# x handed over turned, the reciprocal root applied behind the projections, and a third of the weight rests moved to GpSimd

## The chip, the cores and the metric

The kernel runs on one core of a Trainium2 chip. The metric is the device time of one execution in microseconds (us). The kernel before takes 575.78 us, the median of three runs (575.1 to 575.89).

Five engines work side by side and meet at semaphores: TensorE (PE in the rows; PEld is its loading of weights), VectorE (DVE), ScalarE (ACT), GpSimd (POOL) and SyncE (SP), which here only starts transfers. Each takes its instructions in the order in which the program gives them.

## The reference, cut to what matters

One layer (512 tokens, width 1024): RMSNorm, one input projection, three groups of heads, one output projection, then a SwiGLU block. All data is float32.

```python
def hybrid_layer(x, ...):
    hn = rms_norm(x, g_pre_mix)      # x * rsqrt(mean(x*x) + 1e-6) * g
    proj = hn @ w_in
    mq, mk, mv, fq, fk, fv, f_logit, cvb, cvc, cvh = jnp.split(proj, SPLIT_IDX, axis=-1)
    moba = moba_attention(heads(mq, 6), heads(mk, 6), heads(mv, 6), rel_bias)
    log_f = jax.nn.log_sigmoid(f_logit + b_f)
    fox = forgetting_attention(heads(fq, 6), heads(fk, 6), heads(fv, 6), log_f)
    conv = cvb * causal_depthwise_conv3(cvc * cvh, conv_w)
    mixed = jnp.concatenate([merge(moba), merge(fox), conv], axis=-1) @ w_out
    x = x + rms_norm(mixed, g_post_mix)
    h2 = rms_norm(x, g_pre_ffn)
    ff = (silu(h2 @ w_gate) * (h2 @ w_up)) @ w_down
    return x + rms_norm(ff, g_post_ffn)
```

The root in the first norm is one number per token; g is one number per feature. So `hn @ w_in` is also `r * ((x * g) @ w_in)` with r per token, which is what the change uses.

## The kernel before, in words

Float32 products are made out of two rounded parts. Every operand is split into `hi` (rounded, made by ScalarE, or by GpSimd for the value weights) and `lo` (the rest, made by VectorE), and a product is three products on TensorE: hi*hi, hi*lo, lo*hi (`product`, L1663 to L1668). The splits are called `split(u)`: u counts units of weights, 0 to 2 are chunks of the value weights, 3 to 23 are 1024x128 slices of `w_in`, then come the slices of `w_out` and those of the SwiGLU weights. Units travel through four buffers `raw`, loaded by SyncE when the unit four places earlier has its `lo`.

The opening (up to the first logits) handles one tile of 128 tokens after another: ScalarE squares and takes the root (L752, L754), VectorE multiplies by the reciprocal root and g (`normalise`, L1126), TensorE turns the tile (`turn`, L1702), ScalarE and VectorE make `hn_hi` and `hn_lo` (L770, L1134) out of PSUM. TensorE then makes the values of the tile (`v_mm`, L1720, 128x390 outputs), and in between the four small products of the relative bias (L1688, L1690). g reaches all partitions through a product with a row of ones (L1681). Last come the q and k groups of the first pair of heads.

Attention works on six pairs of heads, three of the moba kind and three of the fox kind (forgetting attention), in 8 steps a pair; a step g is one head and one tile of 128 queries. At each step TensorE makes the logits (L1803, L1805), then three eighths of a projection group of the next pair as filler, then the product with the values where a head is complete (`pv`, L1827, in steps 2 and 6 of a pair) and the transposes of the probabilities of step g - 2 (L1815). VectorE adds the bias (L1297), makes `pT_lo` (L1231), scales the probabilities (L1331), and evacuates groups that are complete; ScalarE makes exp (L859), `pT_hi` (L806) and the splits. A pair's q group is complete in its step 2 and the k group in step 5: ScalarE writes the `hi` halves (L790, two instructions of 64 partitions), VectorE the `lo` halves (L1191, two). TensorE's first logits of the next pair wait for the k group and for two transfers that swap the halves of q (GpSimd's queue, L638 and L640). GpSimd also masks the bias of the fox pairs (L666, one block each) and starts the transfers of the bias. In the last pair the filler is the convolution's groups (`conv_tail`).

The order on each engine is written out by hand in the step loops; there is no scheduler. Behind attention come the output projection, the norms and the SwiGLU block, none of which the change touches beyond the names of the waits.

## Time and profile before

| what | value |
|---|---|
| time, median of 3 runs | 575.78 us |
| the profiled execution | 576.57 us |
| its span | 574.8 us |
| granted clock, mean | 0.998 |
| TensorE busy | 567.5 us, 99% |
| VectorE busy | 471.5 us, 82% |
| ScalarE busy | 319.7 us, 56% |
| GpSimd busy | 110.4 us, 19% |
| first logits of attention | 42.61 us |

The span runs from the first to the last instruction; the time of the execution has 1.8 us around it. A busy TensorE is not one at its peak, because matmuls are pipelined: of two products in a row the second starts long before the first ends. Their pitch, start to start, is the cost of one. In a timeline row the two first numbers are the start and the length in us; at its end stands the idle time of the engine before it and what ended it.

### The profile page before, as it was taken

The numbers are of one execution on the slowest core, as the hardware profiler recorded it, in microseconds if no ns is written. First come the engines' busy times: TensorE is split into PE (matmuls) and PEld (weight loads), VectorE is DVE, ScalarE is ACT, GpSimd is POOL, SyncE is SP. The second block draws the span as 40 slices with busy tenths as digits, with TensorE's granted clock in tenths as the row PEclk, the third lists the DMA queues.
The fourth block names the chain that finished last, engine by engine and source line by source line (L and its number), as shares of the span: only waits on it lengthen the run. The fifth ranks groups of instructions, "written<-read, shape, count | busy, mean of one in ns | idle before, by whom it ended". The sixth has DMA issues, their size and how long they took to land.

```text
span 574.8 us, 9664 instructions
## 1 busy us (share of the span) xinstructions
PE 567.5 (99%) x3372; PEld 502.8 (87%) x3372; DVE 471.5 (82%) x791; ACT 319.7 (56%) x539; POOL 110.4 (19%) x129
## 2 busy tenths in 40 slices
PE   8999999999999999999999999999999999999996
PEld 6988888888888888899999999999999988888884
DVE  5647888888797954799888988988898788888787
ACT  5625765766555645575545546454554565547762
POOL 3020001103220000000324242332324002233100
PEclk9999999999999999999999999999999999999999
DMA  8274334346312471302323223242322359999743
GB/s 331 85 214 136 91 105 132 95 141 185 110 48 100 147 299 68 111 38 75 144 76 131 88 75 144 73 145 74 144 75 81 138 188 268 269 211 199 167 146 146
DMA packets 23144, 78.92 MB, mean 137 GB/s; under 512 B 2972, under 2 KB 2972, under 8 KB 23114
## 3 DMA queue, kind: packets, MB, share of 16 engines
q1 hardware_dynamic: 16716, 57.44, 28.2%
q0 software_dynamic: 6304, 21.00, 16.1%
q8 instruction: 17, 0.28, 0.2%
q10 hardware_dynamic: 94, 0.09, 0.0%
q14 instruction: 13, 0.11, 0.0%
HBM read 71.16 MB, written 4.22 MB: 131 GB/s over the span
## 4 chain that ended last, share of the span: by engine, by line
PE 99%; DVE 0%; POOL 0%; issue 0%; DVEq 0%; ACT 0%; POOLq 0%
PE bank L1666 11%; PE bank L1668 11%; PE bank L1667 11%; PE bank L1951 8%; PE bank L1950 8%; PE bank L1949 8%; PE bank L1957 7%; PE bank L2019 6%; PE bank L2017 6%; PE bank L2015 6%; PE bank L1960 3%; PE bank L1720 3%; PE bank L1827 3%; PE bank L1815 2%; PE bank L1805 1%; PE bank L1803 1%
## 5 line engine op out<-in xcount | busy, mean ns | idle before, releaser
L1950 PE MATMUL bank<-tok_lo,form_hi 128*128 128x256 f32 x320 | 90.6, 283 | 0.0
L1951 PE MATMUL bank<-tok_hi,form_lo 128*128 128x256 f32 x320 | 90.6, 283 | 0.0
L1949 PE MATMUL bank<-tok_hi,form_hi 128*128 128x256 f32 x320 | 90.5, 283 | 0.0
L1666 PE MATMUL bank<-hn,w_hi 128*128 128x512 f32 (+1 forms) x200 | 76.6, 383 | 0.0
L1668 PE MATMUL bank<-hn,w_lo 128*128 128x512 f32 (+1 forms) x200 | 75.0, 375 | 0.0
L1667 PE MATMUL bank<-hn,w_hi 128*128 128x512 f32 (+1 forms) x200 | 74.6, 373 | 0.0
L1949 PEld LDWEIGHTS bank<-tok_hi,form_hi 128*128 128x128 f32 x320 | 60.9, 190 | 1.9
L1951 PEld LDWEIGHTS bank<-tok_hi,form_lo 128*128 128x128 f32 x320 | 61.1, 191 | 0.0
L1950 PEld LDWEIGHTS bank<-tok_lo,form_hi 128*128 128x128 f32 x320 | 61.0, 191 | 0.0
L2015 PE MATMUL bank<-dw_hi,da_hi 128*128 128x512 f32 x154 | 59.9, 389 | 0.0
L2019 PE MATMUL bank<-dw_hi,da_lo 128*128 128x512 f32 x154 | 59.9, 389 | 0.0
L2017 PE MATMUL bank<-dw_lo,da_hi 128*128 128x512 f32 x154 | 59.9, 389 | 0.0
L1957 PE MATMUL bank<-hn,form_hi 128*128 128x512 f32 x160 | 58.1, 397 | 0.0
L712 POOL TENSOR_TENSOR sum_f<-raw 128x512 f32<-128x512 f32 x18 | 27.8, 1544 | 144.9 <-DVE form_lo L1457 144.9
L1457 DVE TENSOR_TENSOR form_lo<-sum_f,form_hi 128x1024 fp32r<-128x1024 f32 x40 | 48.6, 1216 | 0.0
L1457 DVE TENSOR_TENSOR form_lo<-raw,form_hi 128x1024 fp32r<-128x1024 f32 (+1 forms) x40 | 47.0, 1175 | 0.6
L859 ACT ACTIVATE probs<-logits,neg_max 128x128 f32<-128x128 f32 (+3 forms) x48 | 27.1, 564 | 36.4 <-DVE neg_max L1297 36.4
L971 ACT CAST form_hi<-sum_f 128x1024 fp32r<-128x1024 f32 x40 | 42.0, 1053 | 6.2 <-DVE sum_f L1395 5.9
L1960 PE MATMUL bank<-hn,form_lo 128*128 128x256 f32 x160 | 44.9, 281 | 0.0
L1668 PEld LDWEIGHTS bank<-hn,w_lo 128*128 128x128 f32 x200 | 37.7, 188 | 7.2
L1666 PEld LDWEIGHTS bank<-hn,w_hi 128*128 128x128 f32 x200 | 37.7, 189 | 6.1 <-issue 0.9
L1667 PEld LDWEIGHTS bank<-hn,w_hi 128*128 128x128 f32 x200 | 37.8, 189 | 5.1
(206 smaller groups left out, 1397.0 us busy)
## 6 DMA issues: line engine op xcount, KB each, us to landing
raw<-in_w_gate_units SPq DMA_DIRECT2D x22, 512.0 KB, 3.6
raw<-in_w_up_units SPq DMA_DIRECT2D x22, 512.0 KB, 4.5
raw<-in_w_in_units SPq DMA_DIRECT2D x21, 512.0 KB, 3.3
down_x<-in_w_down POOLq DMA_DIRECT2D x15, 512.0 KB, 9.7
down_y<-in_w_down SPq DMA_DIRECT2D x10, 512.0 KB, 9.2
raw<-in_w_out SPq DMA_DIRECT2D x8, 512.0 KB, 3.2
q_lh<-q_hl POOLq DMA_DIRECT2D x12, 256.0 KB, 2.8
down_x<-in_w_down SPq DMA_DIRECT2D x5, 512.0 KB, 3.9
```

The source lines that it names most:

```text
L1457: nc.vector.tensor_tensor(form_lo[par][:, sl, :, :], src, form_hi[par][:, sl, :, :], ALU.subtract).then_inc(form_lo_done, 1)
L1666: nc.tensor.matmul(out_ap, sh, mh, start=first, stop=False)
L1667: nc.tensor.matmul(out_ap, sh, ml, start=False, stop=False)
L1668: return nc.tensor.matmul(out_ap, sl, mh, start=False, stop=last)
L1949: nc.tensor.matmul(out_ap, sh, mh, start=first and k == 0, stop=False, skip_group_check=True)
L1950: nc.tensor.matmul(out_ap, sh, ml, start=False, stop=False, skip_group_check=True)
L1951: mm = nc.tensor.matmul(out_ap, sl, mh, start=False, stop=k == HK - 1, skip_group_check=True)
L1957: nc.tensor.matmul(bank[:, bank_no, :], form_hi[par][:, form, k, :], h2_hl[:, k0 + k, 0, :, :].rearrange("p two n -> p (two n)"), start=fi ...
L1960: mm = nc.tensor.matmul(bank[:, bank_no, 0:HALF], form_lo[par][:, form, k, :], h2_hl[:, k0 + k, 0, 0, :], start=False, stop=k == HK - 1, s ...
L2015: nc.tensor.matmul(out_ap, sh[:, k, tokens_of], mh[:, j, :], start=first and DOWN_CHAIN[n][1], stop=False, skip_group_check=True)
L2017: nc.tensor.matmul(out_ap, sh[:, k, tokens_of], ml[:, j, :], start=False, stop=False, skip_group_check=True)
L2019: return nc.tensor.matmul(out_ap, sl[:, k, tokens_of], mh[:, j, :], start=False, stop=last, skip_group_check=True)
```

## The change

- x comes a second time, turned (`x_t`, features on partitions), in four pieces `X_CHUNKS`. `hn` is now x*g without the root: ScalarE makes `hn_hi` from SBUF with g as a scale for each partition, VectorE `hn_lo`. The transposes of x, the norm row on TensorE and `normalise` are gone. The row tiles of x are still loaded, later, for the squares.
- The values run over features instead of tiles of tokens: `V_CHUNKS` is 1, 3 and 4 slices of 128 features, all four token tiles at each slice, in four banks. The weight rests of the last chunk stand behind the k group.
- The reciprocal root r is spread over columns (`r_tok`, turned by TensorE into `r_open`, copied to `r_cols`). Whatever comes out of a projection is multiplied by r when it is evacuated. For values that is folded in; the copies `vT` and `conv_c` become products; the convolution gets a product more (`conv_y` times `r_cols`); and q and k groups are first scaled into an SBUF tile `qk_t` by VectorE (`scaled_qk`), from which ScalarE and VectorE then make the halves.
- ScalarE's halves of q and k stand behind the `pT_hi` copy of their step, where they stood before it.
- The rests of the units 9, 12, 15, 18 and 21 are made by GpSimd (`rest`), not by VectorE. Who waits for them waits for `pool_lo_done`.

TensorE's order in the opening, before (the identity `ident`, the norm row `g_row`, turned tiles `xn`, values `wv_hi` and `wv_lo`):

```order
L1675 MATMUL bank<-ident 128x128 x4
L1681 MATMUL bank<-g_row,f_one 128x512 x2
L1675 MATMUL bank<-ident 128x128 x2
L1702 MATMUL bank<-ident,xn 128x128 x8
L1720 MATMUL bank<-wv_hi,hn 128x390 x2
L1702 MATMUL bank<-ident,xn 128x128 x8
L1720 MATMUL bank<-wv_hi,hn 128x390 x13
L1720 MATMUL bank<-wv_lo,hn 128x390 x4
L1720 MATMUL bank<-wv_hi,hn 128x390 x9
```

and now:

```order
L1747 MATMUL bank<-ident 128x128 x12
L1780 MATMUL bank<-wv_hi,hn 128x390 x8
L1780 MATMUL bank<-wv_lo,hn 128x390 x4
L1780 MATMUL bank<-wv_hi,hn 128x390 x8
L1780 MATMUL bank<-wv_lo,hn 128x390 x4
L1753 MATMUL bank<-onehot_r,relb_hl 6x512
L1755 MATMUL bank<-onehot_r,relb_hl 6x128
L1780 MATMUL bank<-wv_hi,hn 128x390 x32
L1740 MATMUL bank<-hn,w_hi_69 128x512
L1741 MATMUL bank<-hn,w_hi_69 128x512
L1742 MATMUL bank<-hn,w_lo_73 128x512
```

The values now start right behind twelve transposes of the identity, and 32 value products stand in one piece behind the relative bias.

ScalarE in the steps 5 to 7 of the first pair, before (`pT_hi` the turned probabilities, `k_hl` the k group of the next pair):

```order
L749 CAST w_hi_71<-raw_66 128x1024
L806 CAST pT_hi<-bank 128x4x128
L859 ACTIVATE probs_86,row_sum<-logits,neg_max 128x384
L790 ACTIVATE k_hl_100<-bank 64x512 x2
L806 CAST pT_hi<-bank 128x128
L859 ACTIVATE probs_87,row_sum<-logits,neg_max 128x512
L815 COPY o_top<-bank 64x512
```

and now:

```order
L796 CAST w_hi_71<-raw_66 128x1024
L855 CAST pT_hi<-bank 128x4x128
L907 ACTIVATE probs_86,row_sum<-logits,neg_max 128x384
L855 CAST pT_hi<-bank 128x128
L839 ACTIVATE k_hl_104<-qk_t 64x512 x2
L907 ACTIVATE probs_87,row_sum<-logits,neg_max 128x512
L864 COPY o_top<-bank 64x512
```

The k halves have moved behind the `pT_hi` copy of one block, whose input TensorE makes at the end of that step.

VectorE at the same place, before:

```order
L1231 TENSOR_TENSOR pT_lo<-bank,pT_hi 128x4x128
L1110 TENSOR_TENSOR w_lo_75<-raw_66,w_hi_71 128x1024
L1200 TENSOR_SCALAR f_z<-bank,bf_c 6x512
L1329 RECIPROCAL row_inv<-row_sum 128x1
L1331 TENSOR_SCALAR probs_86<-probs_86,row_inv 128x384
L1191 SCALAR_TENSOR_TENSOR k_hl_100<-bank,k_hl_100 64x512 x2
L1297 ISA logits,neg_max<-bank,bias 128x512
```

and now:

```order
L1303 TENSOR_TENSOR pT_lo<-bank,pT_hi 128x4x128
L1197 TENSOR_TENSOR qk_t<-bank,r_cols 128x512
L1272 TENSOR_SCALAR f_z<-bank,bf_c 6x512
L1403 RECIPROCAL row_inv<-row_sum 128x1
L1405 TENSOR_SCALAR probs_86<-probs_86,row_inv 128x384
L1263 SCALAR_TENSOR_TENSOR k_hl_104<-qk_t,k_hl_104 64x512 x2
L1368 ISA logits,neg_max<-bank,bias 128x512
```

The split of unit 9 is gone and the scaling into `qk_t` stands in its place; the k halves read `qk_t`.

The diff, cut to its core (the declarations of tiles and semaphores and the renamed waits are left out):

```diff
-V_GROUPS = (0, 1, 2, 5)
+V_GROUPS = (2, 3, 4, 5)
...
-V_CHUNKS = ((0, 2), (2, 5), (5, 8))
+V_CHUNKS = ((0, 1), (1, 4), (4, 8))
+X_CHUNKS = ((0, 1), (1, 2), (2, 4), (4, 8))
+LATE_CHUNK = 2
...
+POOL_RESTS = (9, 12, 15, 18, 21)
+
+
+def rests_before(u):
+
+    return u - sum(v < u for v in POOL_RESTS)
...
+        def wait_rest(engine, u):
+
+            if u in POOL_RESTS:
+                engine.wait_ge(pool_lo_done, POOL_RESTS.index(u) + 1)
+            else:
+                engine.wait_ge(lo_done, rests_before(u + 1))
...
-            load_open(0)
-            load_open(1)
+            def load_turned(n):
+                c = slice(*X_CHUNKS[n])
+                sp.dma_start(xt[:, c, :], x_t[:, c, :]).then_inc(xt_in[n], 16)
+
+            load_turned(0)
             load_values(0)
+            load_turned(1)
             load_values(1)
+            load_turned(2)
             load_values(2)
-            load_open(2)
-            load_open(3)
+            load_turned(3)
             load(3, unit(w_in_units, 0))
-            load(4, unit(w_in_units, 1), 1)
...
+            nc.gpsimd.memset(r_tok[:, :, :], 1.0).then_inc(ones_set, 1)
...
+                if u == LATE_CHUNK:
+                    pool.wait_ge(tables_in, 32)
+                    pool.wait_ge(after_set, 1)
+                    nc.gpsimd.tensor_copy(onehot_r[:, :], onehot[:, :]).then_inc(rel_hi_done, 1)
+                    nc.gpsimd.tensor_copy(relb_hl[:, 0, :], relb[:, :]).then_inc(rel_hi_done, 1)
...
+            def rest(u):
+
+                hi, lo = split_slot(u)
+                pool.wait_ge(hi_done, u + 1 - V_UNITS)
+                nc.gpsimd.tensor_tensor(lo[:, :, :], staged(u), hi[:, :, :], ALU.subtract).then_inc(pool_lo_done, 1)
...
             pool.wait_ge(rel_copied, 2)
             pool.dma_start(rel_rows.ap(), rel_row[:, :]).then_inc(rel_out, 16)
             for p in range(MOBA_PAIRS + 1):
                 load_bias(p)
-                if p >= 1:
-                    swap(p)
+                swap(p)
+                if p:
+                    rest(3 * p + 6)
+                if p == 0:
+                    pool.wait_ge(proj_done, V_GROUPS[-1] + 1)
+                    pool.wait_ge(r_open_done, 1)
+                    nc.gpsimd.tensor_copy(r_cols[:, :], r_open[:, :]).then_inc(r_cols_done, 1)
...
+                if p + 1 < PAIRS:
+                    rest(3 * p + 9)
...
+            def tokens_hi(k):
+
+                chunk = next(n for n, (k0, k1) in enumerate(X_CHUNKS) if k0 <= k < k1)
+                act_e.wait_ge(xt_in[chunk], 16)
+                nc.scalar.activation(hn_hi[:, k, :], xt[:, k, :], ACT.Copy, scale=g_feat[:, k:k + 1]
+                                     ).then_inc(hn_hi_done, 1)
...
-                    last = nc.scalar.activation(dst[0:DH, h, :], bank[DH * h:DH * (h + 1), PROJ[G % 2], :], ACT.Copy,
+                    last = nc.scalar.activation(dst[0:DH, h, :], qk_t[DH * h:DH * (h + 1), :], ACT.Copy,
...
-            squares_of(0)
-            squares_of(1)
-            tokens_hi(0)
-            tokens_hi(1)
-            squares_of(2)
-            squares_of(3)
+            act_e.wait_ge(g_in, 16)
+            for k in range(4):
+                tokens_hi(k)
             act_e.wait_ge(rel_done, 1)
             nc.scalar.copy(rel_row[:, 0:SEQ], bank[0:N_MOBA, REL_BANKS[0], :]).then_inc(rel_copied, 1)
             nc.scalar.copy(rel_row[:, SEQ:REL], bank[0:N_MOBA, REL_BANKS[1], 0:REL - SEQ]).then_inc(rel_copied, 1)
-            evac_hi(V_GROUPS[0])
-            tokens_hi(2)
+            for k in range(4, KT):
+                tokens_hi(k)
             split(3)
-            evac_hi(V_GROUPS[1])
-            tokens_hi(3)
+            for t in range(TT):
+                squares_of(t)
             nc.scalar.preload_act_table_set("natural_log_exp_and_others")
             split(4)
-            evac_hi(V_GROUPS[2])
             split(5)
+            act_e.wait_ge(r_turned, 1)
+            nc.scalar.copy(r_open[:, :], bank[:, R_BANK, :]).then_inc(r_open_done, 1)
             evac_hi(group(0, 0))
             split(6)
             evac_hi(group(0, 1))
...
-                if g >= 1:
-                    for G in finished(g - 1):
-                        evac_hi(G)
...
+                if g == 20:
+                    act_e.wait_ge(r_cols_done, 1)
+                    nc.scalar.activation(r_cols2[:, :], r_cols[:, :], ACT.Square).then_inc(r_cols2_done, 1)
                 if g >= 2:
                     evac_pT(g - 2)
+                if g >= 1:
+                    for G in finished(g - 1):
+                        evac_hi(G)
...
+            def tokens_lo(k):
+
+                dve.wait_ge(hn_hi_done, k + 1)
+                nc.vector.scalar_tensor_tensor(out=hn_lo[:, k, :], in0=xt[:, k, :], scalar=g_feat[:, k:k + 1],
+                                               in1=hn_hi[:, k, :], op0=ALU.mult, op1=ALU.subtract
+                                               ).then_inc(hn_lo_done, 1)
+
...
+            def row_scales(t):
+
...
+                if t == 0:
+                    dve.wait_ge(ones_set, 1)
+                nc.vector.tensor_scalar(r_tok[:, t, :], r_tok[:, t, :], rstd[:, SQ1, t:t + 1], None, ALU.mult
+                                        ).then_inc(r_tok_done, 1)
+
+            def scaled_qk(G):
+
+                _, p, j = kind_of(G)
+                dve.wait_ge(proj_done, G + 1)
+                if 2 * p + j:
+
+                    dve.wait_ge(qk_lo_done, 2 * p + j)
+                if p == 0:
+                    dve.wait_ge(r_open_done, 1)
+                elif p == 1:
+                    dve.wait_ge(r_cols_done, 1)
+                nc.vector.tensor_tensor(qk_t[:, :], bank[:, PROJ[G % 2], :], (r_cols if p else r_open)[:, :], ALU.mult
+                                        ).then_inc(proj_read, 1)
...
+                    nc.vector.tensor_tensor(conv_c[:, :], src, r_cols2[:, :], ALU.mult).then_inc(proj_read, 1)
...
+                    nc.vector.tensor_tensor(conv_y[:, :], conv_y[:, :], r_cols[:, :], ALU.mult
+                                            ).then_inc(conv_scaled, 1)
...
+                    for m in range(MOBA_PAIRS):
+                        last = nc.vector.scalar_tensor_tensor(
+                            out=v_moba[:, m, p, :, DH:P],
+                            in0=src[:, P * m:P * (m + 1)].rearrange("p (h d) -> p h d", h=2),
+                            scalar=rstd[:, SQ1, p:p + 1], in1=v_moba[:, m, p, :, 0:DH], op0=ALU.mult,
+                            op1=ALU.subtract)
+                    last.then_inc(v_lo_done, 1)
+                    nc.vector.tensor_scalar(f_tok[:, p, :], src[:, MOBA_W:V_COLS], rstd[:, SQ1, p:p + 1], None,
...
+                    nc.vector.tensor_tensor(vT[:, :], src, r_cols[:, :], ALU.mult).then_inc(proj_read, 1)
...
-                            out=dst[DH:P, h, :], in0=src[DH * h:DH * (h + 1), :], scalar=SCALE if j == 0 else 1.0,
+                            out=dst[DH:P, h, :], in0=qk_t[DH * h:DH * (h + 1), :], scalar=SCALE if j == 0 else 1.0,
                             in1=dst[0:DH, h, :], op0=ALU.mult, op1=ALU.subtract)
-                    last.then_inc(proj_read, 1)
+                    last.then_inc(qk_lo_done, 1)
...
-            normalise(0)
-            normalise(1)
             tokens_lo(0)
             split(0)
             tokens_lo(1)
+            split(1)
+            tokens_lo(2)
             dve.wait_ge(rel_hi_done, 2)
             nc.vector.tensor_tensor(relb_hl[:, 1, :], relb[:, :], relb_hl[:, 0, :], ALU.subtract).then_inc(rel_lo_done, 1)
-            split(1)
+            for k in range(3, KT):
+                tokens_lo(k)
             split(2)
-            normalise(2)
-            normalise(3)
-            evac_lo(V_GROUPS[0])
-            tokens_lo(2)
-            evac_lo(V_GROUPS[1])
-            tokens_lo(3)
             split(3)
-            evac_lo(V_GROUPS[2])
+            for t in range(TT):
+                row_scales(t)
             split(4)
             split(5)
+            scaled_qk(group(0, 0))
             evac_lo(group(0, 0))
             split(6)
+            scaled_qk(group(0, 1))
             evac_lo(group(0, 1))
-            evac_lo(V_GROUPS[3])
+            for t in range(TT):
+                evac_lo(V_GROUPS[t])
...
-                    if not has_hi(G):
+                    if has_hi(G):
+                        scaled_qk(G)
+                    else:
                         evac_lo(G)
                 if s != 7:
                     for G in hi_kinds:
                         evac_lo(G)
                 if g <= STEPS:
                     for u in splits_at(g - 1):
-                        split(u)
+                        if u not in POOL_RESTS:
...
+            for u in range(V_UNITS):
+                pe.wait_ge(wv_hi_done, u + 1)
+                for k in range(*V_CHUNKS[u]):
+                    pe.wait_ge(hn_hi_done, k + 1)
+                    for t in range(TT):
                         v_mm(t, k, hn_hi, wv_hi, k == 0, False)
+                    pe.wait_ge(hn_lo_done, k + 1)
+                    for t in range(TT):
+                        v_mm(t, k, hn_lo, wv_hi, False, False)
+                    if u < LATE_CHUNK:
+                        pe.wait_ge(lo_done, u + 1)
+                        for t in range(TT):
+                            v_mm(t, k, hn_hi, wv_lo, False, False)
+                if u == LATE_CHUNK - 1:
+                    relative_rows()
+            pe.wait_ge(rel_copied, 2)
+            for k in range(KT):
+                proj_step(group(0, 0), V_UNITS, k)
+                if k == 3:
+                    row_scales()
+            for k in range(KT):
+                proj_step(group(0, 1), V_UNITS + 1, k)
+            pe.wait_ge(lo_done, LATE_CHUNK + 1)
+            for t in range(TT):
+                for k in range(*V_CHUNKS[LATE_CHUNK]):
+                    mm = v_mm(t, k, hn_hi, wv_lo, False, k == KT - 1)
+                mm.then_inc(proj_done, 1)
```

## Rows read from the trace of the kernel before

**Rows 1.** The page, chain of work that ended last: share by engine.

```profile
PE 99%; DVE 0%; POOL 0%; issue 0%; DVEq 0%; ACT 0%; POOLq 0%
```

**Rows 2.** Waits of TensorE's weight loads, 42 to 200 us: total, times, longest.

```profile
PEld bank L1827 <- DVE pT_lo L1231: 1.4, 4, 0.4
```

**Rows 3.** Timeline of TensorE, 0 to 43 us: start, length, instruction.

```profile
1.93 1.11 PE L1675 MATMUL bank<-ident 128*128 128x128 f32 x4 [1.93 <-POOL ident L622]
...
7.16 1.92 PE L1702 MATMUL bank<-ident,xn 128*128 128x128 f32 x8
...
27.30 0.47 PE L1666 MATMUL bank<-hn,w_hi 128*128 128x512 f32 x1
...
38.30 3.04 PE L1720 MATMUL bank<-wv_hi,hn 128*128 128x390 f32 x16
...
42.61 0.22 PE L1803 MATMUL bank<-k_hl,q_hl 128*128 128x128 f32 x1
```

**Rows 4.** L1720's weight loads, 11 to 13 and 13 to 15 us: ns min/median/max.

```profile
L1720 PEld LDWEIGHTS bank<-wv_hi,hn x7: 188/330/338, 11.3 to 13.0; 128*128 128x128 f32 x7
...
L1720 PEld LDWEIGHTS bank<-wv_hi,hn x8: 187/190/192, 13.0 to 15.0; 128*128 128x128 f32 x8
```

**Rows 5.** Timeline of GpSimd in the opening.

```profile
0.85 0.51 POOL L618 MEMSET f_one<- 6x512 f32 x1
...
7.85 0.84 POOL L632 CAST wv_hi<-wv_raw 128x780 fp32r<-128x780 f32 x1 [1.05 <-DMA wv_raw<-in_w_v]
```

**Rows 6.** Timeline of ScalarE in the opening.

```profile
4.22 1.06 ACT L752 ACTIVATE squares<-x_open 128x1024 f32<-128x1024 f32 x1 [0.78 <-DMA x_open<-in_x]
...
5.61 1.04 ACT L752 ACTIVATE squares<-x_open 128x1024 f32<-128x1024 f32 x1
...
17.63 0.58 ACT L835 COPY rel_row<-bank 6x512 f32<-6x512 f32 x1 [2.58 <-PE bank L1690]
```

**Rows 7.** Groups of VectorE by shape, 42.5 to 190 us: busy, mean ns, idle.

```profile
L1110 DVE TENSOR_TENSOR w_lo<-raw,w_hi 128x1024 fp32r<-128x1024 f32 x18 | 21.9, 1214 | 0.1
...
L1331 DVE TENSOR_SCALAR probs<-probs,row_inv 128x512 f32<-128x512 f32 x12 | 5.9, 495 | 0.4
...
L1158 DVE SCALAR_TENSOR_TENSOR conv_y<-conv_u,conv_w_c,conv_y 128x512 f32<-128x512 f32 x4 | 3.0, 752 | 0.1
...
L1185 DVE COPY vT<-bank 128x512 f32<-128x512 f32 x3 | 2.0, 679 | 0.0
```

**Rows 8.** Timeline at the end of pair 3, fox kind.

```profile
134.70 1.18 ACT L790 ACTIVATE k_hl<-bank 64x512 fp32r<-64x512 f32 x2
...
136.07 1.39 DVE L1191 SCALAR_TENSOR_TENSOR k_hl<-bank,k_hl 64x512 fp32r<-64x512 f32 x2
...
136.41 0.59 ACT L806 CAST pT_hi<-bank 128x512 fp32r<-128x512 f32 x1 [0.52 <-PE bank L1815]
...
138.75 0.48 PE L1803 MATMUL bank<-k_hl,q_hl 128*128 128x512 f32 x1
```

**Rows 9.** Timeline at the end of pair 0, moba kind.

```profile
62.25 0.27 ACT L806 CAST pT_hi<-bank 128x128 fp32r<-128x128 f32 x1 [1.00 <-PE bank L1815]
...
64.72 0.31 PE L1803 MATMUL bank<-k_hl,q_hl 128*128 128x128 f32 x1
```

**Rows 10.** Timeline in pair 3 and at pair 5's start.

```profile
131.25 0.56 DVE L1297 CUSTOM_DVE_ANT_0 logits<-bank,bias 128x384 f32<-128x384 f32 x1 [0.60 <-POOL bias L666]
...
134.41 0.50 PE L1827 MATMUL bank<-pT_hi,v_fox 128*128 128x512 f32 x1
...
163.54 0.69 DVE L1297 CUSTOM_DVE_ANT_0 logits<-bank,bias 128x512 f32<-128x512 f32 x1 [0.66 <-PE bank L1805]
```

**Rows 11.** GpSimd's sums and masks; VectorE's rests, 254 to 452 us.

```profile
L712 POOL TENSOR_TENSOR sum_f<-raw x18: 1287/1534/1807, 271.9 to 441.8; 128x512 f32<-128x512 f32 x18
...
L666 POOL TENSOR_SCALAR_AFFINE_SELECT bias<-bias x24: 290/296/1483, 106.2 to 185.3; 128x128 f32<-128x128 f32 x24
...
L1457 DVE TENSOR_TENSOR form_lo<-raw,form_hi 128x512 fp32r<-128x512 f32 x20 | 22.5, 1124 | 0.0
```

208 lines of the change are left out of this document (68 added, 140 removed).

## The prediction

> **What bounds the kernel now.** I read the page first: TensorE is busy for 99% of the span and is 99% of the chain that ended last [rows 1]. So only what makes TensorE start sooner, do less or wait counts. The waits of its weight loads between 42 and 200 us are next: 1.4 us in four waits for `pT_lo` [rows 2]. Attention is dense but has four places with no slack at all. The timeline of TensorE before 43 us shows where it does no useful work: transposes of the identity from 1.93 us, the norm row, the first transposes of x at 7.16 us; the first logits of attention come at 42.61 us [rows 3]. Two values of one product matter: weight loads before the value products take 330 ns between 11 and 13 us and 188 ns between 13 and 15 us [rows 4]. The page grants the clock as 1.00 throughout, but the durations are in two classes, and I read them as the lower and the upper level (1.2 and 2.4 GHz). The pitch of these products is 0.335 us early; sixteen of them at 38.30 us take 3.04 us, so (3.04 - 0.33)/15 = 0.18 us later [rows 3]. The rows on the landing of the weights and on ScalarE say what feeds the opening [rows 5, 6], the bodies of VectorE what its edits cost [rows 7], and the timelines at the end of a pair what waits there [rows 8 to 10].
>
> **The opening, step by step.** GpSimd now sets `r_tok` (512 columns) before the identity. The only row of that width is `f_one`, 0.51 us [rows 5], so TensorE starts 0.5 us later, at 1.93 + 0.5 = 2.4 us. Twelve transposes at the pitch of the first eight, (1.92 - 0.42)/7 = 0.21 us [rows 3], end at 5.0. The first chunks have landed by then: 0.26 MB of x and 0.2 MB of weights stand in front, where the first 0.5 MB of x before was read by ScalarE at 4.22 us [rows 6]. Chunk 0 of the values is 12 products; all at 0.335 they take 4.0 us, to 9.0; at 0.18 they would end at 7.2. Chunk 1 needs 1.3 MB to have landed; before, 1.45 MB had by 7.85 us [rows 5], so about 7.3, and a cast of 780 columns takes 0.84 [rows 5], so one of 1170 takes 1.3, to 8.6. I take 9.0 for its start. Then 36 products, 6.6 us, to 15.6; the four small products of the relative bias, some 0.65 us, to 16.2. Now comes a new wait. ScalarE stands in `rel_done` before `tokens_hi(4)`: a copy of 512 columns (0.58 us [rows 6]), a short one and a 128x512 conversion of about the same 0.6 must pass, so TensorE idles about 1.5 us, to 17.7. The 32 products of chunk 2 end at 23.6. The q group is 24 products at 0.228 us (48 of them fill 27.30 to 38.30 [rows 3]), 5.5 us, and four transposes of `r_tok`, 0.5; the k group 5.5 more: 35.1. The rests of chunk 2 (16 x 0.18) end at 38.0.
>
> Beside this, ScalarE makes conversions until 19.2, one split, four squares with their roots at a pitch of 1.39 us (4.22 to 5.61 [rows 6]), to 25.7, then a table, two splits of 1024 columns (a pass of that width is 1.06 [rows 6]) and the copy of the turned roots: 29.6. VectorE's rests for it just precede each group (23.4 against 23.6; 29.3 against 29.6), and I cost these at nothing; a late one costs what it is late. After the k group: the scaling 0.65, the ScalarE halves 1.2, the VectorE halves 1.4 [rows 8], with hand-overs 3.6 us, to 38.8. The first logits stand at 38.8 to 38.9, against 42.61: the opening gives 3.8 us. Bounds: 5.4 if chunk 0 runs at the upper level and chunk 1 lands as early; 2.5 if landings or the root chain are over a microsecond later. VectorE's twelve value rests of 128 columns lie between its k half and its first logits; by the line through 679 ns for 512 and 1214 for 1024 columns [rows 7] they are 0.28 each, 3.4 us. TensorE asks for what follows them only 5 us after logits 0, so that is hidden.
>
> The early rows show what the level costs, not what raises it: TensorE had run transposes and four row products from 1.93 on and was still at 330 ns at 11 us [rows 3, 4]. The Trainium skill ("TensorE: Matmul & The Clock Gate", section Part 4: PE-mode transpose) says that transposes do not count as busy for the gate. The trace agrees as far as it goes. By that rule the twelve transposes warm nothing and chunk 0 costs its 4.0 us; were it false, 7.2, with chunk 1 still not cast before 8.6.
>
> **Attention: the evacuation of q and k.** Before, ScalarE read k's group out of PSUM in the seventh step ahead of the `pT_hi` copy; now VectorE first scales into `qk_t`, and ScalarE's k halves stand behind that copy, which waits for the transposes at the end of that step. Everything behind is serial: the copy, two k halves (1.18 to 1.20), two VectorE halves (1.39), and TensorE's first logits of the next pair wait for the last. In fox pair 3 the copy starts at 136.41 us and hands over after about 0.5; 136.9 + 1.2 + 1.4 + 0.15 for hand-overs = 139.7, where TensorE came at 138.75 [rows 8]: a wait of 1.0 us. Pair 4 has the same rows: 0.9. In a moba pair the copy is one block (0.27 us, hands over after 0.17): 62.25 + 0.17 + 1.2 + 1.4 + 0.15 = 65.2 against 64.72 [rows 9], 0.5 us; pairs 1 and 2 alike, 0.4 and 0.5. Sum over the five turns: 3.3 us. Bounds: VectorE's halves now have both inputs in SBUF; the nearest rows are 752 ns for 128x512 with two inputs there and 495 for one input [rows 7]. With 752 the sum is 3.7, with 500, and ScalarE's halves as fast, the chain drops under 2.5 us and the pauses vanish: 0.
>
> **Attention: VectorE's balance.** The five removed splits give back 1.21 each, 6.1 us; ten scalings of 0.68 (the copy `vT<-bank` takes 679 ns for the same width; that copy and `conv_c`'s become products at no extra) and two for the convolution, 8.1 us. Busy time barely moves, but place counts. TensorE's four waits are for `pT_lo` ahead of a value product [rows 2, 10], and removed splits stand behind it. In pair 5 the convolution's added product (0.6) lies before it, and VectorE enters the pair 1.15 us later against TensorE, of which the 0.66 idle before logits 40 absorbs part [rows 10]: 0.6 + 0.5 = 1.1 us more at that pair's first value product. In pair 3 the scaling of step 3 pushes the q halves by 0.6; GpSimd's swap and mask follow them, and VectorE already waits 0.60 for that mask [rows 10]: 0.6 more at 134.41, and 0.3 at the pair's earlier value product. Pairs 1 and 4 give 0.1 each: in them VectorE's idle time in steps 3 and 4 takes the scaling up. Sum 2.2, bounds 0.5 and 4.
>
> **GpSimd's rests.** 128x512 takes 1287 to 1807 ns there [rows 11], so a rest is 2.6 to 3.6 us against 1.21 on VectorE. Each is wanted only a step or more later (unit 18: started about 135.1 after the last mask of pair 3, done by 138.7, mask for pair 4 by 139.0, wanted by VectorE at about 140.9), and the stores that wait for them too; cost 0. Without that cover, 1 to 2 us per fox turn. A mask of 128x128 takes 296 ns and at most 1483 [rows 11], the long ones where a VectorE split runs, while VectorE's 128x512 rests beside GpSimd's sums take 1124 on average against 679 for a copy of that width [rows 7, 11]: both sides lose. The Trainium skill ("SBUF — State Buffer", section Who interferes with whom) says that a VectorE instruction with two SBUF inputs and a GpSimd one that reads SBUF exclude each other for the whole instruction. That is the rival below.
>
> **Sum.** The profiled execution is 576.57 us over a span of 574.8; the median shown is 575.78, 0.8 lower. -3.8 + 3.3 + 2.2 = +1.7: 578.3 by the profiled one, 577.5 by the median. Under 0.2%, 1.15 us, is what a measurement of this kernel can't tell from no change.
>
> **Rivals.**
> A, the forecast: 577.5, its own range 576.5 to 579.5. Chance 0.47.
> B, faster: the k turn stays hidden, because halves read from SBUF run near the 495 ns of the scaled probabilities [rows 7] rather than 590 and 695 (half of 1.18 and 1.39 [rows 8]). Place: ScalarE's and VectorE's k halves at each turn; it decides where copy, halves and hand-overs together are below the 2.5 us that TensorE needs from those transposes to the next logits. Then -3.8 and +1.6 of the other waits: 573.6. Against it: the 495 has one tensor input, and 752 is the row with two from SBUF [rows 7]. Chance 0.25 (an opening of 5.4 with few `pT_lo` waits counts here).
> C, no change: the k pauses are right, but VectorE regains its lag in them, so the `pT_lo` waits stay at 1.4: -3.8 + 3.3 = -0.5, 575.3. For it: idle time like the 0.66 [rows 10] grows with each pause of TensorE. Chance 0.18 (to 0.20 with the edges of A).
> D, much slower: by the exclusion, GpSimd's rests of 18 and 21 run into the k halves of the fox turns and hold them for what is left of 3 us, and pair 4's first mask comes late: 1 us more in each of two turns, and the opening at 2.5: +5.0, 580.8. Chance 0.10.
> That the change doesn't do what it says: the products and transposes removed are gone from the program; no chance kept.
> Slower: A and D less an edge, 0.55; same 0.20; faster 0.25. The range for 8 in 10 is 573.3 to 580.0: it takes most of B and C, all of A.
>
> **What would show it.** Logits 0 at 38.3 to 39.3 us. TensorE idle of about 1.5 us near 16.2, released by `hn` of ScalarE. At the start of pairs 1 to 5 waits of 0.4 to 0.6 (moba) and 0.9 to 1.1 us (fox) for `k_hl` of VectorE, which is B's test: none there, and I am wrong. Waits for `pT_lo` of 3 to 4 us in all, the longest in pair 5. VectorE's halves from SBUF at 690 to 750 ns. From 200 us on nothing longer or shorter than before.

## The result, and the profile after

The changed kernel takes 580.89 us (median of 4 runs, 580.22 to 581.63) against 575.67 us before: slower by 5.2 us, ratio 1.0088 with a 95% interval of 1.0075 to 1.0100. The forecast was 577.5 with a range from 573.3 to 580.0. The sign was right, the size was not.

Where the time went can be read from eight stages, cut at the first logits of each pair (the first TensorE row `bank<-k_hl,q_hl` of the pair) and at the first product of the output projection. All numbers are lengths in us, each from the one profiled execution of its kernel; e2, e8, e11 and e14 are experiments below.

| stage | before | changed | e2 | e8 | e11 | e14 |
|---|---|---|---|---|---|---|
| opening, to logits 0 | 42.61 | 41.27 | 39.45 | 42.57 | 37.42 | 37.68 |
| pair 0 | 22.11 | 22.67 | 22.22 | 22.44 | 22.23 | 22.19 |
| pair 1 | 24.67 | 25.57 | 24.53 | 25.35 | 24.50 | 24.50 |
| pair 2 | 24.48 | 24.71 | 24.23 | 24.61 | 24.24 | 24.20 |
| pair 3 | 24.88 | 26.64 | 25.45 | 26.03 | 24.75 | 24.72 |
| pair 4 | 24.04 | 24.95 | 24.08 | 24.89 | 23.76 | 23.76 |
| pair 5 | 29.50 | 30.80 | 30.64 | 30.00 | 29.56 | 29.52 |
| output projection to end | 382.51 | 383.29 | 383.30 | 382.51 | 383.34 | 382.53 |

The changed kernel gains 1.34 in the opening and loses 4.36 in pairs 0 to 4, 1.30 in pair 5 and 0.78 behind: +5.10, the difference of the spans (579.9 against 574.8).

TensorE's share of the chain that ended last, 99% before [rows 1], in the page's part 4:

```profile
PE 85%; DVE 7%; issue 3%; ACT 3%; DMA 1%; POOL 1%; DVEq 0%; SPq 0%; ACTq 0%; POOLq 0%
```

And who held up its weight loads between 40 and 210 us (in total, times, longest; [rows 2] has 1.4 us):

```profile
PEld bank L1855 <- DVE pT_lo L1303: 4.9, 7, 1.6
PEld bank L1831 <- DVE k_hl L1263: 4.1, 6, 1.0
PEld bank L1740 <- DVE ext_lo L1161: 0.8, 1, 0.8
```

Three kinds of wait: the one for `k_hl` is new, those for `pT_lo` have grown by 3.5 us, and `ext_lo` (a w_out unit's rest) is one that no term of the forecast held. The waits in the pairs grew by 6.6 us and the stages by 5.66; two waits of the kernel before (0.39 and 0.40 us at 80.80 and 105.54 us, which the trace puts down to "issue") are gone in the changed kernel and make up most of that difference.

**The opening.** TensorE to 44 us, the timeline that answers [rows 3]:

```profile
2.39 2.82 PE L1747 MATMUL bank<-ident 128*128 128x128 f32 x12 [2.39 <-POOL ident L658]
5.53 1.70 PE L1780 MATMUL bank<-wv_hi,hn 128*128 128x390 f32 x8 [0.32 <-POOL wv_hi L668]
...
9.54 1.69 PE L1780 MATMUL bank<-wv_hi,hn 128*128 128x390 f32 x8 [1.59 <-POOL wv_hi L668]
...
18.90 7.47 PE L1780 MATMUL bank<-wv_hi,hn 128*128 128x390 f32 x32 [1.54 <-ACT hn L818]
...
37.60 3.02 PE L1780 MATMUL bank<-wv_lo,hn 128*128 128x390 f32 x16
41.27 0.33 PE L1831 MATMUL bank<-k_hl,q_hl 128*128 128x128 f32 x1 [0.65 <-DVE k_hl L1263]
```

The pause of 1.54 us stands where the forecast put it (1.5 us, released by ScalarE's `hn`). But the 32 products behind it need 7.3 us where 5.9 were forecast. Busy time by engine, granted clock, DMA share and GB/s in three stretches say why:

```profile
16.00:19.00 3.00, 1.46 (x9) 0.74 (x9) 0.21 (x1) 1.59 (x4) 0.56 (x1) 1.00 1.02 408
19.00:22.00 3.00, 3.00 (x10) 3.00 (x11) 3.00 (x5) 3.00 (x5) 0.15 (x1) 0.51 0.90 345
22.00:26.00 4.00, 4.00 (x23) 4.00 (x22) 3.37 (x8) 3.90 (x10) 1.13 (x2) 0.94 0.41 144
```

The granted clock is 0.51 between 19 and 22 us, the lower of the two levels (1.2 GHz), behind a stretch in which TensorE was busy for 1.46 of 3 us.

**The turn of a pair.** The end of pair 3, the timeline of all engines that answers [rows 8]:

```profile
135.78 2.39 POOL L682 TENSOR_TENSOR w_lo<-raw,w_hi 128x1024 fp32r<-128x1024 f32 x1
...
136.29 2.03 DVE L1405 TENSOR_SCALAR probs<-probs,row_inv 128x256 f32<-128x256 f32 x1
...
137.63 0.59 ACT L855 CAST pT_hi<-bank 128x512 fp32r<-128x512 f32 x1 [1.62 <-PE bank L1843]
138.12 1.27 ACT L839 ACTIVATE k_hl<-qk_t 64x512 fp32r<-64x512 f32 x2
...
139.42 1.38 DVE L1263 SCALAR_TENSOR_TENSOR k_hl<-qk_t,k_hl 64x512 fp32r<-64x512 f32 x2 [1.10 <-ACT k_hl L839]
...
140.86 0.19 PEld L1831 LDWEIGHTS bank<-k_hl,q_hl 128*128 128x128 f32 x1 [0.88 <-DVE k_hl L1263]
```

The chain is as forecast: copy, two ScalarE halves, two VectorE halves, first logits. ScalarE has nothing to do for 1.62 us before the copy, with `qk_t` ready since 136.2; that idle time is what the place costs. And a scaling of the probabilities takes 2.03 us beside GpSimd's rest, and ends 0.15 us behind it. The turn of pair 0 (moba kind, [rows 9]) reads the same:

```profile
61.03 0.27 ACT L855 CAST pT_hi<-bank 128x128 fp32r<-128x128 f32 x1 [2.09 <-PE bank L1843]
...
61.20 1.27 ACT L839 ACTIVATE k_hl<-qk_t 64x512 fp32r<-64x512 f32 x2
62.50 1.38 DVE L1263 SCALAR_TENSOR_TENSOR k_hl<-qk_t,k_hl 64x512 fp32r<-64x512 f32 x2 [1.93 <-ACT k_hl L839]
```

VectorE's bodies between 42 and 200 us, the groups that answer [rows 7]:

```profile
L1405 DVE TENSOR_SCALAR probs<-probs,row_inv 128x256 f32<-128x256 f32 x12 | 7.6, 632 | 0.4
...
L1263 DVE SCALAR_TENSOR_TENSOR k_hl<-qk_t,k_hl 64x512 fp32r<-64x512 f32 x10 | 6.9, 685 | 6.9 <-ACT k_hl L839 6.9
L1197 DVE TENSOR_TENSOR qk_t<-bank,r_cols 128x512 f32<-128x512 f32 x10 | 6.8, 680 | 0.0
```

The halves read from SBUF cost 685 ns each, as good as out of PSUM (690). The scaling costs the 0.68 of the forecast. The last number of the second row is the one to stop at: VectorE stood 6.9 us in front of its k halves.

The weight loads that waited in pairs 1 and 5 and at the output projection:

```profile
72.92 0.19 PEld L1855 LDWEIGHTS bank<-pT_hi,v_moba 128*128 128x128 f32 x1 [0.94 <-DVE pT_lo L1303]
...
176.21 0.19 PEld L1855 LDWEIGHTS bank<-pT_hi,v_fox 128*128 128x128 f32 x1 [1.58 <-DVE pT_lo L1303]
...
208.51 0.19 PEld L1740 LDWEIGHTS bank<-ext_hi,cat_hi 128*128 128x128 f32 x1 [0.81 <-DVE ext_lo L1161]
```

### The profile page after: what moved, and what is told of

Read it like the earlier page. It is cut to its first block, busy times and chain, and to the rows that moved or that the text cites. A ratio compares the mean times of both kernels' runs of the same rounds, so it can differ in the third digit from the quotient of the medians.

```text
span 579.9 us, 9629 instructions
## 1 busy us (share of the span) xinstructions
PE 563.2 (97%) x3346; PEld 498.8 (86%) x3346; DVE 476.6 (82%) x804; ACT 322.2 (56%) x541; POOL 124.7 (21%) x136
## 4 chain that ended last, share of the span: by engine, by line
PE 85%; DVE 7%; issue 3%; ACT 3%; DMA 1%; POOL 1%; DVEq 0%; SPq 0%; ACTq 0%; POOLq 0%
PE bank L1979 8%; PE bank L1978 8%; PE bank L1977 8%; PE bank L1740 8%; PE bank L1742 8%; PE bank L1741 8%; PE bank L1985 6%; PE bank L2047 6%; PE bank L2043 6%; PE bank L2045 6%; PE bank L1988 3%; PE bank L1855 2%; PE bank L1780 2%; PE bank L1843 2%; ACT k_hl L839 1%
```

## Experiments

Times are medians. "Before" is the kernel before, run beside each group of experiments on the same chip (575.4 to 575.7 us), and each ratio is to that. e1, e2, e3 and e5 form one group, e4, e6, e7 and e8 the second, e9 to e13 the third, e14 and e15 the fourth; between groups the medians of the kernel before differ by up to 0.3 us, which a difference of two medians then holds as well.

**1. The pause in the opening** (e1). From the changed kernel, ScalarE's order:

```diff
+            for k in range(4, KT):
+                tokens_hi(k)
             act_e.wait_ge(rel_done, 1)
             nc.scalar.copy(rel_row[:, 0:SEQ], ...)
             nc.scalar.copy(rel_row[:, SEQ:REL], ...)
-            for k in range(4, KT):
-                tokens_hi(k)
```

> The changed kernel with ScalarE's last four conversions of hn (features 512 to 1023) put ahead of its two copies of the relative bias; all else as changed. In the changed kernel TensorE stands still for 1.54 us before the last 32 value products and these then take 7.3 us (0.228 each) where 0.18 to 0.20 was seen before; the granted clock reads 0.51 between 19 and 22 us. Theory: the pause itself lowers the granted clock. Then both go: the products start at about 17.4 us and take 5.8 to 6.4 us, first logits near 38.6 instead of 41.3, time 580.9 - 2.5 = 578.4 us, clock 1.00 throughout. Rival: the slow products are due to something beside them (transfers at 0.9 of the DMA engines, ScalarE and VectorE writing hn). Then only the pause goes: 32 products in 7.3 us again, 579.4 us.

Measured 578.97 us, ratio to before 1.0057 [1.0044, 1.0070], 1.9 us less than the changed kernel. TensorE and the clock:

```profile
17.35 6.03 PE L1780 MATMUL bank<-wv_hi,hn 128*128 128x390 f32 x32
...
38.26 0.33 PE L1831 MATMUL bank<-k_hl,q_hl 128*128 128x128 f32 x1 [0.66 <-DVE k_hl L1263]
```

```profile
19.00:22.00 3.00, 3.00 (x19) 3.00 (x18) 1.92 (x5) 2.94 (x8) 0.21 (x1) 1.00 1.04 398
```

Pause and low clock are both gone, and logits 0 come 3.0 us earlier. The DMA engines are as busy as in the changed kernel and ScalarE nearly so; VectorE is less (1.92 instead of 3.00 us). What speaks most against the rival is e2: it has the same pause and VectorE and ScalarE as busy as in the changed kernel (3.00 us each of the 3 us from 18.40 on), and in its profile, as in that of e3, the 32 products take 5.99 us at a granted clock of 1.00. So work beside them isn't what makes the products slow, and the pause costs the clock in some executions only.

The median falls by 1.9 and not by 3. Part of it is that spread. Another part stands at the output projection of this profile, 384.13 us instead of 383.29:

```profile
202.01 1.05 ACT L796 CAST ext_hi<-raw 128x1024 fp32r<-128x1024 f32 x1 [2.69 <-DMA raw<-in_w_out]
...
206.36 0.19 PEld L1740 LDWEIGHTS bank<-ext_hi,cat_hi 128*128 128x128 f32 x1 [1.63 <-DVE ext_lo L1161]
```

A w_out unit landed late (ScalarE waited 1.73 us for it in the changed kernel), and TensorE's wait for its rest is 1.63 instead of 0.81 us. In e6, which reaches the output projection still earlier, that stage is back at 383.27 us.

**2. The place of the halves** (e2; e8 is its mirror on the kernel before). e2, from the changed kernel:

```diff
+                if g >= 1:
+                    for G in finished(g - 1):
+                        evac_hi(G)
                 if g >= 2:
                     evac_pT(g - 2)
-                if g >= 1:
-                    for G in finished(g - 1):
-                        evac_hi(G)
```

> The changed kernel with ScalarE's halves of q and k put back ahead of the pT_hi copy of their step; they still read the scaled tile qk_t. Theory: the place behind the copy is what makes TensorE wait at each pair's start (0.43, 0.44, 0.51, 0.88 and 0.87 us in the changed kernel, 3.1 in all). Then these waits go, at most 0.4 comes back as later pT_lo, and the time is 580.9 - 2.7 to - 3.1 = 577.8 to 578.2 us. Rival: the added scaling on VectorE makes the chain late by itself, or VectorE's lag, since in pairs 3 and 4 one scaling of the probabilities (128x256, 0.42 us elsewhere) takes 2.03 us beside GpSimd's rest and would now stand ahead of VectorE's k halves. Then the two fox turns keep 0.5 us or more each and the time is 579 to 580 us.

Measured 576.61 us, 1.0022 [1.0013, 1.0031]: 4.3 us less than the changed kernel, more than the theory asked. TensorE's waits between 42 and 200 us:

```profile
PEld bank L1855 <- DVE pT_lo L1303: 3.5, 5, 1.4
```

No wait for `k_hl` is left in any turn of a pair, and the waits for `pT_lo` that stood at 72.92 and 122.94 us (0.94 and 0.44) are gone too: with VectorE no longer standing at its k halves, the next pair's work behind them in its queue comes in time.

e8 makes the opposite edit alone on the kernel before (in its step loop, where `evac_hi` reads PSUM):

> The kernel before with one edit of the change alone: ScalarE's halves of q and k stand behind the pT_hi copy of their step. Neither the scaling nor the opening nor GpSimd's rests are in it. Theory: the order alone costs what mending it gave back (4.3 us): waits for k_hl of 0.4 to 0.9 us at the starts of pairs 1 to 5 and about 1 us more for pT_lo; 575.6 + 4.3 = 579.9 us, at least 578.6. Rival: the order only costs together with the scaling on VectorE; then 575.6 to 577 us.

Measured 579.38 us, 1.0059 [1.0045, 1.0074]: +3.6 us.

```profile
PEld bank L1827 <- DVE pT_lo L1231: 2.9, 5, 0.9
PEld bank L1803 <- DVE k_hl L1191: 2.7, 5, 0.8
```

Among the waits for `pT_lo` are the same two as in the changed kernel, 0.90 and 0.44 us, without any scaling.

From both sides: the order of two instructions on ScalarE, which was 56% busy, is 3.6 to 4.3 of the 5.2 us. The scaling isn't needed for it.

**3. GpSimd's rests** (e3 off the changed kernel, e4 onto the kernel before; e13, off the mended one, is in part 5).

```diff
-POOL_RESTS = (9, 12, 15, 18, 21)
+POOL_RESTS = ()
...
```

> The changed kernel with the rests of units 9, 12, 15, 18 and 21 back on VectorE; GpSimd makes none. Theory: GpSimd's rests cost the path little, because what they hold up on VectorE (two scalings of the probabilities, 2.03 instead of 0.42 us) lies in the shade of the k halves; five splits of 1.21 us come back into VectorE's queue, pT_lo waits grow from 4.6 by 1 to 3 us, time 582 to 584 us. Rival (the exclusion of GpSimd and VectorE is what the change paid for): without it the waits of TensorE in the fox pairs shrink, time 578.5 to 580 us.

Measured 580.68 us, 1.0093 [1.0080, 1.0106]: no difference to the changed kernel. Neither side was right; the splits come back at next to no cost (pair 1 takes 25.78 us instead of 25.57, every other pair the same within 0.02), and what GpSimd had held up was covered.

e4 puts the same `POOL_RESTS`, `rest` and `wait_rest` into the kernel before:

> The kernel before with the rests of units 9, 12, 15, 18 and 21 made by GpSimd, at the places where the changed kernel has them; nothing else of the change. Theory: VectorE's five splits of 1.21 us were in the shade of TensorE, and so are GpSimd's of 2.4: no change, 575.0 to 576.0 us, although one scaling of the probabilities at each fox turn takes 2.0 instead of 0.4 us beside them. Rival: at the fox turns there is no slack before the change (VectorE's k halves stood right behind that scaling), so 1.6 us late at pairs 4 and 5: 576.5 to 578.5 us.

Measured 576.35 us against 575.74, 1.0007 [0.9998, 1.0016]: no difference that the times can tell. The profile shows one: pair 5 takes 29.91 us instead of 29.50, with a wait for `pT_lo` of 0.71 instead of 0.29 at 171.12 us, so in the kernel before GpSimd's rests seem to cost 0.4 us. What GpSimd holds up is there too, in the group of VectorE's scalings of the probabilities (367 ns before):

```profile
L1357 DVE TENSOR_SCALAR probs<-probs,row_inv 128x256 f32<-128x256 f32 x12 | 7.7, 640 | 0.4
```

Its profile shows a third thing. The opening is the kernel before's own, yet logits 0 come at 41.32 us and not at 42.61, since the products reach the upper level earlier:

```profile
9.93 1.04 PE L1728 MATMUL bank<-ident,xn 128*128 128x128 f32 x8
10.72 2.57 PE L1746 MATMUL bank<-wv_hi,hn 128*128 128x390 f32 x13
```

In the kernel before's profile the same rows are

```profile
9.78 1.91 PE L1702 MATMUL bank<-ident,xn 128*128 128x128 f32 x8
11.34 3.24 PE L1720 MATMUL bank<-wv_hi,hn 128*128 128x390 f32 x13
```

so 42.61 us is what one execution had, not a property of the kernel.

**4. Without the scaling** (e5). From the changed kernel with e2's order, `scaled_qk` is not called, and `evac_hi` and `evac_lo` read the bank:

```diff
-                    last = nc.scalar.activation(dst[0:DH, h, :], qk_t[DH * h:DH * (h + 1), :], ACT.Copy,
+                    last = nc.scalar.activation(dst[0:DH, h, :], bank[DH * h:DH * (h + 1), PROJ[G % 2], :], ACT.Copy,
...
```

> The changed kernel with q and k evacuated straight out of PSUM as before the change (ScalarE's halves ahead of the pT_hi copy, no tile qk_t); the reciprocal root is left out of q and k, all other products with it stay. It shows what the opening alone is worth and what the scaling of q and k costs. Theory: the ten scalings of 0.68 us are what makes pT_lo late: the waits at the pairs' starts go (3.1 us), the waits for pT_lo fall from 4.6 to 1.5 to 2.5 us, time 580.9 - 3.1 - 2.5 = 575.3 us, near the kernel before less its gain in the opening (575.7 - 1.4 + 0.6 for the convolution's added product). Rival: the waits for pT_lo come from elsewhere (the later first logits' VectorE work, GpSimd's rests); then 577.5 to 578.5 us.

Measured 576.88 us, 1.0036 [1.0020, 1.0052]: as e2 (576.61), which has the scalings. The low clock struck e5 more often (7 of 9 executions at a mean of 0.995 or under, 3 of 11 in e2), so the stages are the better comparison: the six pairs take 141.3 us in e5 and 141.2 in e2. Ten scalings, 6.8 us of VectorE, cost nothing that shows once the order is right. Pair 3 is 0.6 us shorter without them; pairs 0 to 2 together are 0.7 longer, with waits of 0.47, 0.38 and 0.40 us before a projection product that e2 doesn't have. The scaling frees the PSUM bank before the halves are made, which would explain these; no run shows it. The waits for `pT_lo` fell only from 3.5 to 2.9 (pair 3's), and 1.44 us in pair 5 stayed. So "the scalings make pT_lo late" is refuted but for pair 3.

**5. Both orders, then the waits that are left** (e6, e7, e10, e11, e13). e6 has the edits of e1 and e2:

> The changed kernel with both orders of ScalarE mended: the last four conversions of hn ahead of the copies of the relative bias, and the halves of q and k ahead of the pT_hi copy. Theory: the two gains of 1.9 and 4.3 us add up: 580.9 - 6.2 = 574.7 us, first logits at 37.6 to 38.3 us, waits for pT_lo 3.5 us. Rival: TensorE arriving earlier finds VectorE and the transfers of w_out where they were, and part of it is waited away again in pair 5 and at the output projection: 575.5 to 576.5 us.

Measured 574.24 us, 0.9973 [0.9962, 0.9984]: the gains add up (6.65 us against 6.2), and it beats the kernel before by 1.5 us. e7, from e6, moves the convolution's product, in `conv_tail`:

```diff
-                    dve.wait_ge(conv_step, 4 * c + 4)
-                    nc.vector.tensor_tensor(conv_y[:, :], conv_y[:, :], r_cols[:, :], ALU.mult
-                                            ).then_inc(conv_scaled, 1)
                 else:
+                    dve.wait_ge(conv_step, 4 * c + 4)
+                    nc.vector.tensor_tensor(conv_y[:, :], conv_y[:, :], r_cols[:, :], ALU.mult
+                                            ).then_inc(conv_scaled, 1)
                     dve.wait_ge(conv_scaled, c + 1)
```

> The kernel of the run with both orders mended, and the convolution's added product (conv_y times the root, 0.69 us) moved from behind the taps to just ahead of conv_o, so that it stands behind the pT_lo for which TensorE waits in pair 5. Theory: the wait of 1.44 us in pair 5 falls by the 0.6 to 0.7 us of that product, to about 0.8; the time falls by 0.6 us against that run, 574.1 us if that run has 574.7. Rival: VectorE has no slack behind either, so that the next wait (0.27 at the last value product, 0.8 for ext_lo) grows by the same amount and the time stays.

Measured 573.87 us, 0.9961 [0.9947, 0.9974]. Pair 5's first wait falls from 1.43 to 0.69 us and the stage from 30.65 to 29.90; the intervals of the two times overlap, so the 0.37 us of the medians settles nothing, the stage does. e10, from e7, turns round two entries of GpSimd's queue:

```diff
+                mask(p, 1, 2)
                 if p + 1 < PAIRS:
                     swap(p + 1)
-                for i in (2, 1, 0):
+                for i in (1, 0):
                     mask(p, 1, i)
```

> The kernel of the run with the late product, with GpSimd's second mask pass in pairs 3 and 4 turned round: the first mask of the second head ahead of the swap of the next pair's q, which waits for VectorE's q halves. Theory: the wait of 0.95 us for pT_lo at 131 us comes from that mask standing behind the swap (VectorE idles 0.59 us for it, in the changed kernel and before): it falls to about 0.4, the one in pair 4 to 0.2 or less, time 573.9 - 0.6 = 573.3 us. Rival: VectorE is simply full there, the idle time only moves: 573.9 us.

Measured 572.29 us, 0.9942 [0.9929, 0.9956]: 3.1 us under the kernel before where e7 was 1.9 under it, so 1.3 us gained where 0.6 was expected. The stages say the same: pair 3 is 0.68 shorter, pair 4 0.31, and pair 5 another 0.37, where the wait at the first value product falls from 0.69 to 0.32 us. Waits between 42 and 210 us:

```profile
PEld bank L1856 <- DVE pT_lo L1304: 1.3, 4, 0.4
PEld bank L1741 <- DVE ext_lo L1162: 0.9, 1, 0.9
```

e11, from e10, lets ScalarE and VectorE work on different heads:

```diff
-                last.then_inc(proj_hi, 1)
+                    nc.scalar.activation(...).then_inc(proj_hi, 1)      # one for each head
-                    dve.wait_ge(proj_hi, 2 * p + j + 1)
                     for h in range(2):
+                        dve.wait_ge(proj_hi, 2 * (2 * p + j) + h + 1)
...
```

> As the run with the swap behind the mask, and ScalarE signals each head's half of q and k by itself, so that VectorE makes the rest of the first head beside ScalarE's second. Theory: the chain behind the k group in the opening (scaling 0.69, 1.28 on ScalarE, 1.38 on VectorE) gets 0.6 us shorter and the wait before logits 0 (0.66 us) nearly goes: 0.5 to 0.6 us off. Rival: VectorE's instruction that reads the same tile and writes beside it slows ScalarE's, or the hand-overs eat it: under 0.2 us off.

Measured 571.71 us, 0.9935 [0.9922, 0.9949], the fastest kernel with all of the computation in it: 3.7 us under the kernel before and some 9 under the changed one (5.2 and 3.7). The wait before logits 0 falls from 0.98 to 0.34 us. On this kernel the rests go back to VectorE (e13, `POOL_RESTS = ()`):

> As the run by heads, with the rests of units 9, 12, 15, 18 and 21 back on VectorE. In the changed kernel that made no difference (580.7 against 580.9 us). Theory: now that the k halves are early, a scaling of the probabilities held up by 1.6 us beside GpSimd's rest stands on VectorE's way in the fox turns, but VectorE idles there long enough: no difference, within 0.5 us. Rival 1: the hold is paid now, so VectorE's own rests are better by 1 us. Rival 2: the five splits are paid: worse by 1 us.

Measured 573.36 us, 0.9964 [0.9952, 0.9976]: +1.65 us, rival 2. Pair 1 takes 25.91 instead of 24.50, with waits for `k_hl` back. Moving the rests to GpSimd changed nothing in the changed kernel and is worth 1.6 us in the mended one.

**6. The end** (e14, e15). What stood open was the 0.8 us from the output projection on. e14 drops the convolution's products with the root from e11:

> The kernel of the run by heads (571.7 us) without the two products of the convolution with the root; they are left out of the computation. From the output projection's first product to the end every kernel with the change's opening takes 383.3 to 383.5 us, the two without it 382.5; at the output projection TensorE waits 0.8 to 0.9 us for the rest of a w_out unit, 0.2 before. Theory: VectorE has no slack in the last eight steps, and the second product (0.68 us at 188 us) is that wait. Without it that stage takes 382.6 us; the waits of 0.34 and 0.26 us for pT_lo in pair 5 go to 0.3 or less each; time 571.7 - 0.7 to - 1.0 = 570.7 to 571.0 us. Rival: the late rest comes from the landing of its transfer; then the stage stays at 383.3 us and the time at 571.5 us or more.

Measured 571.06 us, 0.9920 [0.9906, 0.9934]. The wait for `ext_lo` is not among the waits any more, and the stage takes 382.53 us, as before the change. e14 drops both products; that it is the second one that costs is read from the trace: behind the first VectorE idles 1.44 and 0.96 us for TensorE (172.50 and 175.82 us in e11), and pair 5 is as long without the two (29.52 against 29.56). e15 keeps the products and gives the second to GpSimd:

```diff
+            pool.wait_ge(conv_step, 8)
+            nc.gpsimd.tensor_tensor(conv_y[:, :], conv_y[:, :], r_cols[:, :], ALU.mult).then_inc(conv_scaled, 1)
...
```

> The kernel of the run by heads, all of the computation in it, with the second of the convolution's two products made by GpSimd, which is idle from 180 to 194 us, instead of VectorE. It has 5 us of time. Theory: VectorE is relieved of 0.68 us in its last steps, the wait for the w_out rest falls from 0.9 to 0.3 us and the time by 0.5 to 0.6, to 571.1 us. Rival: the product (1.3 to 1.8 us on GpSimd, both inputs in SBUF) starts while VectorE makes a w_out rest and runs beside a scaling of the probabilities, which it holds up by up to 1.2 us, and nothing is gained: 571.5 to 572.3 us.

Measured 571.78 us, 0.9932 [0.9918, 0.9946]: nothing gained, the rival:

```profile
182.79 2.19 POOL L741 TENSOR_TENSOR conv_y<-conv_y,r_cols 128x512 f32<-128x512 f32 x1 [2.76 <-DVE conv_y L1223]
```

```profile
183.95 1.19 DVE L1408 TENSOR_SCALAR probs<-probs,row_inv 128x256 f32<-128x256 f32 x1
```

In e11 that scaling took 0.36 us. VectorE saved one product of 0.68 us and lost 0.83 us behind GpSimd.

**7. What keeps the clock up** (e9). From e5, behind `relative_rows()`:

```diff
+                    for _ in range(12):
+                        nc.tensor.transpose(bank[:, R_BANK, 0:P], ident[:, :], ident[:, :])
```

> The kernel of the run with unscaled q and k (the root is left out of q and k), with twelve transposes of the identity put into TensorE's pause before the last 32 value products (behind the relative bias; the products still wait for hn). So far executions of kernels with that pause read a mean granted clock down to 0.994 (8 of 9 of this one are at 0.995 or under), those without it never under 0.997. Theory A: any work in the pause keeps the level; then the clock of all executions is 0.997 or more and the median falls from 576.9 by up to 1.4 us, to 575.5 to 576. Theory B: transposes don't keep it; the clock stays at 0.994 to 0.995 in most executions and the time at 576.9 us.

Measured 576.89 us, 1.0027 [1.0017, 1.0037]. (The expectation counts 8 of e5's 9 executions at 0.995 or under; it is 7.) Of 29 executions with the empty pause (the changed kernel, e2, e3, e5) 12 have a mean granted clock of 0.996 or less (3 us at the lower level take 0.003 off the mean, so some more may hide above that), of 120 without it (61 of the kernel before, 59 of the others) none; with the pause filled, 1 of 11. That speaks for A: transposes keep the level. It is not quite shown, because e9 ran on another chip than e2, e3 and e5, and no kernel with the empty pause ran there. And the time did not fall as A has it:

```profile
17.93 1.53 PE L1796 MATMUL bank<-ident 128*128 128x128 f32 x12
19.53 5.99 PE L1777 MATMUL bank<-wv_hi,hn 128*128 128x390 f32 x32
...
41.18 0.30 PE L1830 MATMUL bank<-k_hl,q_hl 128*128 128x128 f32 x1 [1.22 <-DMA q_lh<-q_hl]
```

The 32 products are fast, and TensorE then waits 1.22 us for the transfer that swaps q, so the 1.4 us would have ended in that wait. That the swap is what hides the clock's cost in this variant rests on this one profile.

## Why the prediction was wrong in size

- **The waits for the k halves: right.** Forecast 0.5, 0.4, 0.5, 1.0 and 0.9, in all 3.3 us; measured 0.43, 0.44, 0.51, 0.88 and 0.87, in all 3.13 (the sixth wait of the 4.1 is the opening's). Rival B fell by its own test: halves from SBUF take 685 ns.
- **The opening: the term that failed most.** Forecast -3.8, measured -1.34. Of the 2.5 us between them 1.4 is the step "the 32 products of chunk 2 end at 23.6", priced at 0.18 each: measured 7.31 us, to 26.2. The forecast had the pause, to 0.04 us, and did not ask what it does to the granted clock, which fell to 0.51. 0.5 is the landing: chunk 1's cast began at 8.32 us and its products at 9.54, where 9.0 was taken. 0.5 is chunk 1 itself, 7.1 us for 36 products priced at 0.18 (a wait of 0.2 for `wv_lo`, and a pitch above 0.2 in the first twelve). Chunk 0 ran at the upper level at once (8 products in 1.70 us), against the 4.0 us of the forecast; that gained nothing, because chunk 1 had not landed, which is what the text had said of that bound.
- **The baseline of that term.** The 3.8 was measured from 42.61 us [rows 3], and the same instructions gave 41.32 in e4. The sum went by the profiled execution throughout, which is consistent, but the level of the early products differs between executions of one kernel, and the bounds should have carried the 1.3 us.
- **pT_lo: half right.** Forecast +2.2, measured +3.5. Pair 5 came as worked out: 1.1 forecast, 1.58 - 0.29 = 1.3 measured at its first value product, and e7 took away the 0.7 of the product's place; 0.26 at the last one was not forecast and is gone in e14. Pair 3 has the right number, 0.9 forecast and 1.0 measured, but only half of it by the mechanism named. Of the 0.6 forecast at the second head's value product 0.95 - 0.43 = 0.5 came, through the scaling (0.41 without it, in e5) and GpSimd's mask behind the swap (e10). The 0.44 at the earlier value product, forecast as 0.3, is the order's: it is gone in e2, which has the scalings, and it is there in e8, which has none. What failed is "Pairs 1 and 4 give 0.1 each: in them VectorE's idle time in steps 3 and 4 takes the scaling up", for pair 1: 0.94 us at 72.92. I had priced the late k chain only by TensorE's wait for it; VectorE waits in it too, 6.9 us over five turns, and all that stands behind its k halves shifts. So the order cost 4.3 and not 3.3.
- **"From 200 us on nothing longer or shorter than before": wrong by 0.78 us.** The convolution's second product stands where VectorE has no slack for the w_out rests; e14 removes both products and with them the whole 0.8 us. I had put a price on the first product only.
- **GpSimd's rests at no cost: right in the changed kernel** (e3), though 2.40 us each were under the forecast's 2.6 to 3.6, and not "both sides lose": every rest took 2.38 to 2.42, VectorE alone lost.
- **Rival D had the right number and the wrong reason.** 580.8 was forecast for "the exclusion" and 580.89 came, by luck. The hold, a scaling of the probabilities kept waiting by GpSimd's rest, is real (2.03 and 2.02 us instead of 0.37), but VectorE still waited 1.10 us for ScalarE's k halves behind it, and taking it away changes nothing (e3). A number that fits is no evidence for its mechanism.

The Trainium skill ("SBUF — State Buffer", section Who interferes with whom) names both kinds of VectorE instruction that take the ports shared with GpSimd: those with two SBUF inputs, and `tensor_scalar` or a copy in a two-port mode. I had drawn only on the first half. The trace agrees with both: the one-input `TENSOR_SCALAR` was held to the end of GpSimd's rest, and the scan with two SBUF inputs took 1.74 us instead of 1.20 beside the rest of 83.65. `qk_t<-bank,r_cols`, with one input in PSUM and one in SBUF, ran its usual 0.68 us at 58.72 us beside the rest of 57.62. By the rule of that page of the Trainium skill, "Whoever issues first gets the shared pair for the whole instruction", the place of a rest against the scaling of the probabilities decides. The runs agree: in e15 GpSimd's product, begun while a VectorE split ran, needed 2.19 us, and the scaling begun behind it was held to its end.

The other page of the Trainium skill that the forecast drew on ("TensorE: Matmul & The Clock Gate", section Part 4: PE-mode transpose) says that transposes don't count as busy in the same way. The changed kernel's trace disagrees: nothing but twelve transposes ran before 5.53 us, in 2.82 us (the same twelve take 1.53 in e9 at the upper level), and the first eight products behind them took 1.70 us, the upper level's pitch. With e9's transposes in the pause the mean clock stayed above 0.996 in 10 of 11 executions. The measurement decides.

## What to carry to other kernels

An in-order engine that is half idle can still hold the path: ask of each instruction what it waits for and what stands behind it, since one that is ready must not stand behind one that isn't (e2: 4.3 us, no instruction more or less). When a late operand makes a second engine wait too, price what is queued there behind the wait, not only the wait of the bound engine. Offloading to GpSimd pays or not by what VectorE does in the same microseconds: nothing in the changed kernel, 1.6 us in the mended one, and nothing for a product beside a scaling that it holds up.

## What the runs showed of the hardware

- **A pause of 1.5 us can halve TensorE's clock for some 3 us behind it**, in some executions and not in others: behind the same pause the 32 products took 7.47 us in the changed kernel and 5.99 in e2, and 12 of 29 executions had the low mean clock. Length alone doesn't decide: pauses of 1.59, 1.41 and 1.95 us before chunk 1 (the changed kernel, e6, e9) were followed by eight products in 1.69 us each time, the upper level, and no kernel that has only that pause showed the low mean clock. The rise is as variable: the first eight value products took 1.70, 2.57, 2.19 and 2.97 us in the changed kernel, e1, e10 and e7, at a granted clock that the view gives as 1.00 in all.
- **VectorE and GpSimd:** the 128x256 scaling of the probabilities took 2.03 and 2.02 us beside GpSimd's rests in pairs 3 and 4 (0.37 before), the scan of two SBUF inputs 1.74 (1.20 before), while the rests, which had begun first, took 2.38 to 2.42 us each. Begun second, GpSimd pays: its product in e15 took 2.19 us, where sums of that shape take 1.29 at least [rows 11]. The wait hides in the busy time of the instruction: no view lists it among the waits, only the mean of the group by shape shows it (632 against 367 ns).
